# Small loads issued by another queue, squares summed per head, and gate products placed between attention units

## Time and profile before

| | |
|---|---|
| median of three runs | 2365.89 us |
| profiled execution | 2365.77 us |
| its span | 2364.0 us |
| TensorE busy | 1976.3 us (84%) |
| VectorE busy | 414.3 us |
| ScalarE busy | 317.9 us |
| DMA waits in the chain that ended last | 33% of the span |
| TensorE in that chain | 60% |

### The profile page before, as it was taken

One profiled execution on the slowest core, in us unless ns is written; L12 is line 12 of the kernel. 1 busy time (PEld: TensorE's weight loads), 2 busy tenths in 40 slices (PEclk: granted clock), 3 DMA queues, 4 the chain that ended last, 5 costly groups with the idle time before them and its releaser, 6 DMA issues.

```text
span 2364.0 us, 27849 instructions
## 1 busy us (share of the span) xinstructions
PE 1976.3 (84%) x12006; PEld 1249.7 (53%) x12006; DVE 414.3 (18%) x1209; ACT 317.9 (13%) x722; POOL 0.2 (0%) x4
## 2 busy tenths in 40 slices
PE   7999998976666666666666699899999999899999
PEld 4468787521111111111111155778888748588888
DVE  5113333300000000000000033451000105620000
ACT  4132021200000000000000022341000103501000
POOL 0000000000000000000000000000000000000000
PEclk9999998978888788787888899999999999999999
DMA  9146576999999999999999973526434645155341
GB/s 350 66 171 222 187 267 244 404 428 429 428 428 429 428 429 428 428 429 428 429 428 428 425 254 127 187 72 236 156 107 161 216 141 196 61 191 188 131 178 36
DMA packets 147871, 648.45 MB, mean 274 GB/s; under 512 B 10645, under 2 KB 17410, under 8 KB 123016
## 3 DMA queue, kind: packets, MB, share of 16 engines
q1 hardware_dynamic: 141254, 643.16, 68.7%
q10 hardware_dynamic: 6530, 4.01, 0.6%
HBM read 646.10 MB, written 1.05 MB: 274 GB/s over the span
## 4 chain that ended last, share of the span: by engine, by line
PE 60%; DMA 33%; DVE 4%; ACT 1%; issue 1%; SPq 1%; ACTq 1%; DVEq 0%
DMA ring<-in_w_exp 32%; PE bank L823 28%; PE bank L837 6%; PE bank L2309 6%; PE bank L1626 4%; PE bank L1378 4%; PE bank L1641 2%; PE bank L856 1%; DMA ring<-in_w_ada 1%; DVE scr L2204 1%; DVE scr L2221 1%; PE bank L593 1%; PE bank L1303 1%; PE bank L701 1%; PE bank L1312 1%
## 5 line engine op out<-in xcount | busy, mean ns | idle before, releaser
L823 PE MATMUL bank<-hx,ring 128*128 128x256 f32 (+1 forms) x2944 | 655.1, 385 | 0.7 <-ACT hx L719 0.7
L823 PEld LDWEIGHTS bank<-hx,ring 128*128 128x128 f32 x2944 | 560.6, 191 | 92.1 <-issue 19.0
L1626 PE MATMUL bank<-ring,arena 128*32 128x512 f32 x1968 | 304.0, 751 | 208.3 <-DMA ring<-in_w_exp 198.0
L1626 PEld LDWEIGHTS bank<-ring,arena 128*32 128x32 f32 x1968 | 60.6, 124 | 434.1 <-DMA ring<-in_w_exp 315.2
L1641 PE MATMUL bank<-ring,arena 128*32 128x512 f32 x1008 | 162.0, 784 | 80.1 <-DMA ring<-in_w_exp 69.2
L837 PE MATMUL bank<-ring,hx 128*128 128x512 f32 (+1 forms) x384 | 152.9, 561 | 1.4 <-ACT hx L779 0.7
L2309 PE MATMUL bank<-arena,ring 128*128 128x256 f32 x704 | 152.4, 380 | 1.6 <-DVE arena L2342 1.6
L2309 PEld LDWEIGHTS bank<-arena,ring 128*128 128x128 f32 x704 | 133.9, 190 | 19.8 <-issue 2.0
L1641 PEld LDWEIGHTS bank<-ring,arena 128*32 128x32 f32 x1008 | 32.9, 132 | 192.1 <-DMA ring<-in_w_exp 111.1
L837 PEld LDWEIGHTS bank<-ring,hx 128*128 128x128 f32 x384 | 72.9, 190 | 80.2 <-issue 76.1
L1684 DVE COPY arena<-bank 128x256 f32<-128x256 f32 x16 | 6.8, 424 | 524.1 <-PE bank L1631 524.1
(11 more groups left out here) (369 smaller groups left out, 1368.7 us busy)
## 6 DMA issues: line engine op xcount, KB each, us to landing
ring<-in_w_exp SPq DMA_DIRECT2D x186, 2048.0 KB, 16.3
ring<-in_w_ada SPq DMA_DIRECT2D x36, 2048.0 KB, 12.1
ring<-in_w_in SPq DMA_DIRECT2D x29, 2048.0 KB, 9.0
ring<-in_w_ffn_in SPq DMA_DIRECT2D x20, 2048.0 KB, 7.9
ring<-in_w_ffn_out SPq DMA_DIRECT2D x10, 2048.0 KB, 7.8
ring<-in_w_out SPq DMA_DIRECT2D x6, 2048.0 KB, 11.9
arena<-in_w_exp SPq DMA_DIRECT2D x4, 2048.0 KB, 20.2
ring<-in_w_up_nsa SPq DMA_DIRECT2D x2, 2048.0 KB, 9.1
```

The lines of the kernel that those rows point to most:

```text
L823: ins = pe.matmul(b[:, o:o + n], w[:, k, j * P:(j + 1) * P], h[:, k, :], start=k == 0, stop=k == KD - 1)
L1626: ins = pe.matmul(banks[s][32 * j:32 * j + 32, :], e_xe[:, 2 * t + kk, :], w[:, kk, 512 * j:512 * j + 512], start=t + kk == 0, stop=t + kk ...
```

## The change

1. The 20 small loads are issued by SyncE, in the tile list behind `branch_ml` and before the two `out1_` tiles, still after the step "full S3". `pe_rope` stands behind the mixer's products instead of before them, and VectorE's copy of its result (`dve_turn_pe`) behind VectorE's side of the mixer. `dve_rope` keeps its place and its wait for the loads.
2. The squares of the mLSTM heads are summed head by head, one fused instruction behind each piece of `hh`; the product and the reduction over all of it are gone.
3. Gate tiles 2 and 3 of each layer are computed in halves of 32 products: the first half of tile 2 where the tile was, the second behind the head transposes, the first half of tile 3 behind the scores of unit 0, the second behind the compressed scores. The transposed compressed keys follow tile 3's first half. ScalarE applies the sigmoid at once to the first half of tile 2; the other three are copied as they are, and one sigmoid over all six blocks follows the last unit. The order of the first units changes on TensorE (compressed transposes, scores 2, turned 0, scores 3, turned 1, values 0), and on VectorE: maxima of unit 0 go into the compression stage, behind the keys' mean, and unit 0 is normed before the compressed softmax.

The core of the diff:

```diff
@@ pe_branches: - pe_rope(pe);  pe program: + pe_rope(pe) behind m_out[0][0](pe)
@@ act_branches
         act_mlstm_head(act, 3)
-        act_second_loads(act)
-        AC.stage("mlstm")
         act.wait_ge(*at("mlstm mean"))
@@ dve_mlstm
-        sq = view(arena, 16804, P, 8, P)
         hf = hh.rearrange("p c h e -> p (c h) e")
-        v.tensor_tensor(sq, hf, hf, ALU.mult).then_inc(*DV.step())
-        v.wait_ge(*DV.last())
-        v.tensor_reduce(w4[:, 0:8], sq, AX, ALU.add).then_inc(*DV.step())
-        v.wait_ge(*DV.last())
@@ dve_mlstm_out, for each head and half
+            v.wait_ge(*DV.last())
+            v.tensor_tensor_reduce(sqo, hh[:, c, h, :], hh[:, c, h, :], 1.0, 0.0, ALU.mult, ALU.add,
+                                   w4[:, 4 * c + h:4 * c + h + 1]).then_inc(*DV.step())
@@ second loads: act.dma_start -> sp.dma_start, the list is unchanged
+    def dve_turn_pe(v):
+        DV.stage("rope")
+        v.wait_ge(*at("full pet"))
+        v.tensor_copy(pet, bank_of("pet")[0:HD, 0:64]).then_inc(*DV.step("free pet", "pe ready"))
@@ pe_compress
-        pe_gates2(pe, l, 2)
+        pe_gate_half(pe, l, 2, 0)
...
         pe_heads(pe, l)
+        pe_gate_half(pe, l, 2, 1)
...
-        pe_gates2(pe, l, 3)
+
+    def pe_ckeys(pe, l):
         pe.wait_ge(*at(f"kdup{l}"))
@@ act_compress
-        act_gates2(act, l, 2)
+        key = f"gt2{l}20"
+        act.wait_ge(*at("full " + key))
+        act.activation(gates[:, 0:2, 1, :], bank_of(key)[:, :].rearrange("p (j t) -> p j t", j=2), ACT.Sigmoid).then_inc(
+            *AC.step("free " + key))
...
+        act_gate_raw(act, l, 2, 1)
         act.wait_ge(*at(f"cmp mean{l}"))
...
-        act_gates2(act, l, 3)
@@ dve_compress, behind "cmp mean"
+        dve_maxima(v, l, 0)
@@ pe_attend
         scores(0)
+        pe_gate_half(pe, l, 3, 0)
+        pe_ckeys(pe, l)
+        scores(1)
         pe.wait_ge(*at(f"kct ready{l}"))
...
-        scores(1)
+        pe_gate_half(pe, l, 3, 1)
         pe.wait_ge(*at(f"scT{l}"))
...
+        scores(2)
         turned(0)
-        scores(2)
+        scores(3)
         turned(1)
         values(0)
-        scores(3)
@@ act_attend
         probs(0)
+        act_gate_raw(act, l, 3, 0)
...
         probs(1)
+        act_gate_raw(act, l, 3, 1)
...
         copies(LAST)
+        act.wait_ge(*AC.last())
+        act.activation(gates[:, 2:8, 1, :], gates[:, 2:8, 1, :], ACT.Sigmoid).then_inc(*AC.step(f"gates{l + 1}"))
@@ dve_attend
-        softmax_in(0)
         softmax_in(1)
         v.wait_ge(*at(f"head gates{l}"))
+        normed(0)
         v.wait_ge(*at(f"full ct{l}"))
...
-        normed(0)
         softmax_in(2)
@@ new helpers
+    def pe_gate_half(pe, l, t, i):
+        w = tile(pe, f"merge2_{l}{t}0")
+        key = f"gt2{l}{t}{i}"
+        b = bank(pe, key)
+        for j in range(2):
+            for k in range(KD):
+                ins = pe.matmul(b[:, j * N:(j + 1) * N], w[:, k, (2 * i + j) * P:(2 * i + j + 1) * P], h2[:, k, :],
+                                start=k == 0, stop=k == KD - 1)
+        ins.then_inc(*PE.step("full " + key))
+        if i:
+            mark_used(pe, f"merge2_{l}{t}0")
+
+    def act_gate_raw(act, l, t, i):
+        key = f"gt2{l}{t}{i}"
+        act.wait_ge(*at("full " + key))
+        blk = 4 * t + 2 * i - KD
+        act.copy(gates[:, blk:blk + 2, 1, :], bank_of(key)[:, :].rearrange("p (j t) -> p j t", j=2)).then_inc(
+            *AC.step("free " + key))
@@ SyncE
-        for n in range(N_PRE - 4):
+        for n in range(N_PRE - 6):
+            one(n, stream[n])
+        sp_second_loads(sp)
+        for n in range(N_PRE - 6, N_PRE - 4):
             one(n, stream[n])
```

More of the change, by code:

```diff
@@ L914, in pe_branches @@
         pe_mlstm_turn(pe)
-        pe_rope(pe)
     def act_conv(act, i):
@@ L1272, in dve_mlstm @@
                 v.scalar_tensor_tensor(o, b[:, h * P:(h + 1) * P], c_mln[:, h:h + 1], o, ALU.mult, ALU.mult).then_inc(*DV.step(f"free mturn{c}", "yb0"))
+    sqo = arena[:, 18340:18468]
     def dve_mlstm_out(v, h):
@@ L1746, in program, with sp_second_loads @@
     GROUPS = [(0, 8, 0, 0), (768, 2, 8, 1), (KW0, 2, 10, 1), (QB0, 8, 12, 2), (QB0 + 512, 8, 20, 3)]
-    def act_second_loads(act):
-        AC.stage("rope")
-        act.wait_ge(*at("full S3"))
+    def sp_second_loads(sp):
+        sp.wait_ge(*at("full S3"))
         def load(dst, src, **kw):
-            act.dma_start(dst, src, **kw).then_inc(*K.load("load_second"))
+            sp.dma_start(dst, src, **kw).then_inc(*K.load("load_second"))
         pos = A["positions_2"]
@@ L1786, in dve_rope @@
         v.wait_ge(*K.loaded("load_second"))
-        v.wait_ge(*at("full pet"))
-        b = bank_of("pet")
-        v.tensor_copy(pet, b[0:HD, 0:64]).then_inc(*DV.step("free pet", "pe ready"))
         v.tensor_tensor(fold, ident[:, 0:32], ident[:, 32:64], ALU.add).then_inc(*DV.step())
@@ L1990, in dve_compress @@
         v.tensor_scalar(msc[0:15, 0:2], msc[0:15, 0:2], 1.0 / HD, EPS, ALU.mult, ALU.add).then_inc(*DV.step(f"cmp mean{l}"))
+        DV.stage("attend")
+        dve_maxima(v, l, 0)
+        DV.stage("compress")
         g = gain_l[0:15, l, 1, :].rearrange("p (s e) -> p s e", s=2)
@@ L2191, in on_dve, with dve_maxima @@
         return par == 1 and m % 3 == 2
+    def dve_maxima(v, l, m):
+        if m >= 3:
+            v.wait_ge(*at(f"full pt{l}_{m - 3}1"))
+        for par in range(2):
+            key = f"s{l}_{m}{par}"
+            v.wait_ge(*at("full " + key))
+            b = bank_of(key)
+            for c, (lo, hi) in enumerate(((0, P), (P, 3 * P))):
+                v.tensor_tensor_reduce(sm[:, m % 3, par, lo:hi], b[:, lo:hi], causal[:, P:N] if c == 0 else causal[:, :],
+                                       -1.0, 3e38, ALU.add, ALU.min, mx[:, m % 3, par, c:c + 1]).then_inc(
+                    *DV.step("free " + key, f"sm{l}_{m}{par}"))
     def dve_attend(v, l):
@@ L2196, in softmax_in @@
         def softmax_in(m):
-            if m >= 3:
-                v.wait_ge(*at(f"full pt{l}_{m - 3}1"))
-            for par in range(2):
-                key = f"s{l}_{m}{par}"
-                v.wait_ge(*at("full " + key))
-                b = bank_of(key)
-                for c, (lo, hi) in enumerate(((0, P), (P, 3 * P))):
-                    v.tensor_tensor_reduce(sm[:, m % 3, par, lo:hi], b[:, lo:hi], causal[:, P:N] if c == 0 else causal[:, :],
-                                           -1.0, 3e38, ALU.add, ALU.min, mx[:, m % 3, par, c:c + 1]).then_inc(
-                        *DV.step("free " + key, f"sm{l}_{m}{par}"))
+            dve_maxima(v, l, m)
         def normed(m):
@@ L2406, in _ @@
         m_out[0][0](pe)
+        pe_rope(pe)
         n_ffn0[0](pe)
@@ L2482, in _ @@
         m_out[0][1](v)
+        dve_turn_pe(v)
         dve_gain(v, "gain ffn0", gs, c_ffn[:, 0:8], adaX[0][:, 32:40], "adaX0b")
```

## The result

The changed kernel took 2339.1 us (median of four runs, 2338.06 to 2343.72) against 2366.02 before, a ratio of 0.9888 with a 95% interval of 0.9877 to 0.99: 26.9 us less. Run again later beside new runs of before it took 2338.4 (2336.6 to 2338.98), ratio 0.9878, 0.9861 to 0.9894. The forecast was 2343.5, a gain of 22.3.

A forecast was written before the change was run, and what follows sets the result against it. DMA bounds the experts' stretch, whose start TensorE's progress sets; the gains lie in TensorE's idle around it. 7.5 us ahead of the experts plus 14.8 in two attentions made 22.3, hence 2343.5 us, own range 2340 to 2348, wide 2337.5 to 2351.

The forecast's parts named there:

- the two places: TensorE's idle holes at the mLSTM's end and each attention's start: 7.5 us ahead of the experts, 7.4 us per layer.
- The root behind its mean: End of the mLSTM: with the loads off ScalarE, the root follows VectorE's mean at once, saving 3.9 us.
- The guess that the table load would come ahead of the wait: ScalarE's root: its table loads before the wait for the mean, saving 3.9 us; behind it, 2.65.
- The wait for small loads: Ahead of the first merge product: TensorE no longer waits for the small loads, saving 2.9 us.
- the half clock at the mixer's start: Mixer's first products: the 2 us clock loss stays; 2 to 3 us more gain if it vanishes, 2 less if doubled.
- the 0.3 of the moved transposes: Between mixer and norm: the position table's two transposes, moved there, cost about 0.3 us.
- The squares: End of the mLSTM: summing squares per head saves 1.0 us net, between 0 and 1.5.
- The attentions: Start of each layer's attention: 9.1 us gained less 1.7 for half clock, 7.4 per layer, range 5.5 to 9.1.
- The joint sigmoid: End of the attention: table load 1.28 us and sigmoid 1.9 stay hidden, with 6 us to spare.
- rival (a): Clock holds through both attention starts, 1.7 us more each, and perhaps 1 at the mixer: 2339 us; chance 17%.
- Rival (d): SyncE's queue fills: 4 us per small load gives 2388 us, slower than before from 2.9 an issue; chance 4%.
- the limit of 375.5: VectorE's angle work: small loads may land as late as 375.5 us before TensorE stalls for a bank.

The follow-up runs named there:

- the second profile: The changed kernel, unaltered, profiled a second time, later; run again later it took 2338.4 us, ratio 0.9878 to before.
- the halved loads: The changed kernel with each of the 20 small loads issued in two halves by partitions, 40 issues on SyncE; 2341.13 us.
- the table ahead: The changed kernel with the position table's transposes and their copy put back ahead of the first merge product; 2343.69 us.
- the three single parts: Three kernels made from before, each with one part of the change: loads 2360.58 us, squares 2367.39 us, gate halves 2351.07 us.
- quarters: The changed kernel with each of the 20 small loads issued in four pieces, 80 issues on SyncE; 2353.39 us.

## Why the prediction came out as it did

The sign and the two places were right, and the forecast was 4.4 us too high: 2339.1 lies just below the forecast's own 2340 to 2348, inside the wide range of 2337.5 to 2351. By its own terms:

- The root behind its mean, 3.9 booked. From the mean to TensorE's start took 361.07 - 356.19 = 4.88 us before and 357.81 - 356.60 = 1.21 after: 3.7 (3.9 in the second profile). The guess that the table load would come ahead of the wait held (347.65).
- The wait for small loads, 2.9 booked: the merge product had started 370.16 - 367.15 = 3.01 us behind the last gated product and now starts 0.26 behind it: 2.75.
- **The term that was mis-sized is the half clock at the mixer's start.** The forecast kept the whole loss, because TensorE would still idle twice for 2 us, and said that 2 to 3 us more would come if it vanished. From head 3 to the experts 9.25 and 10.05 us were gained, not 7.5. The root and the squares gave 4.8 and 5.1 of that (24.18 us from head 3 to L604 before, 19.35 and 19.10 after; 4.9 booked) and the wait 2.75; what is left is 1.7 and 2.2 us, or 2.0 and 2.5 with the 0.3 of the moved transposes. The idles were there (0.78 and 2.10 us, 1.96 and 1.68), but each time only the transposes or the product ran slow, no longer both.
- The squares, 1.0 booked: 1.16 measured between head 3 and the mean (19.30 to 18.14), with eight instructions of 0.29 as the nearest row had it. The forecast did not say that this term hangs on part one; alone it is zero.
- The attentions, 9.1 - 1.7 booked each. In the first layer unit 1 was turned 5.9 us earlier reckoned from the join (6.0 forecast), the idle was 2.34 (2.5), and unit 4's scores came 9.1 and 8.7 earlier (9.7 without the clock's loss). What reached the end was 8.32 and 8.75, then 8.03 and 7.55, against 7.4. The clock's price was about right: where it fell, in three of the four, the rows behind the idle took 1.5 us more than at full clock. But the forecast took off 0.6 us for VectorE's chain and 1.7 for the clock, and these overlap. In the one attention at full clock TensorE waited 0.75 us for VectorE a unit later, and 0.16 at the same place where the clock had fallen (first profile, then second, both in the second layer):

```profile
2008.69 0.98 PE L2090 MATMUL bank<-ident,scr 128*128 128x128 f32 x6 [0.75 <-DVE scr L2236]
```
```profile
2008.53 0.98 PE L2090 MATMUL bank<-ident,scr 128*128 128x128 f32 x6 [0.16 <-DVE scr L2236]
```

- A slip in the sum: 1542.65 - 1533.7 is 8.95, not 9.1, which would have made the forecast 2343.8.
- The joint sigmoid lay beside other work: 1.49 us, begun at 1550.11, against the first merge product at 1554.36.
- The median of the first series hit rival (a)'s 2339, in part by luck. (a) had the clock hold through both attentions and perhaps 1 us at the mixer; it held in one attention of four, and the mixer gave 2.0 to 2.5. And 0.7 and 1.5 us of the gain lies in stretches without an edit: the end of the experts gave 2.2 and 2.0, and the start of the kernel took 1.6 and 0.6 back. So (a) was right about the clock as the direction of the miss, not about the place.
- Rival (d) was not what happened, since an issue cost 0.72 us (14.5 us for 20). The limits behind it held: at 1.34 us a load no bank wait, at 1.9 us a wait of 9.67, with the loads 10.9 us past the limit of 375.5. That the change turns slower than before at 2.9 us a load was not reached. The price of the expert tiles sent later was missing from it.
- The rule of the Trainium skill that the forecast weighed ("DMA: Bandwidth & Descriptors", Queues, rings and completion order: one ring's descriptors are taken in order) agrees with the trace. The first loads behind the weights landed 8.4 to 10.9 us after issue, at 358.3 to 359.4, with the branch weights landed at 359.1; those issued from 357.5 us on took 2.2 to 3.5. It cost nothing, as said.

Open stays the tail of the experts: from last tile to join 11.12 us before and 8.75 in both profiles of after, in code that no edit touches. This is nearly all of the 2.0 to 2.2 us by which experts to join is shorter. The same 16 products take 3.64 us at half clock or 1.92 at full there. Of the ten profiles of kernels with parts one and three together eight had 8.75 (the others 10.3 with the halved loads, 10.2 with the table ahead), while before and the three single parts all had over 11. The length of the idle ahead of the last tile does not decide it: 2.99 us stood there with the products at full clock (second profile), 1.89 with them at half (before). The cause stays open.

## What to carry to other kernels

Where an engine waits behind a list of issues, what is computed ahead of the wait is worth nothing until the issues are gone: undo the larger cause first, then measure the smaller. Fill ahead of a place where a wait ends, and move the filler's copy out of PSUM along with it, or the bank that it holds becomes the next wait. Where an idle is left, cut a smaller piece: a quarter of 3.6 us in an idle of 2.34 paid. Price each idle removed with the half clock that may follow it. When small transfers move to the queue that feeds a DMA-bound stretch, count the time in which that queue sends no weights, even if everything that waits for the small ones is covered.

## What the runs showed of the hardware

- The issue of a small load does not cost SyncE in proportion to its size: 0.46 us for 128 KB, 0.43 for most of 8 and 32 KB, 1.22 for one of 1 KB; halves mostly 0.60, quarters 0.42, with single ones up to 1.4.
- A table load that stands ahead of the wait cost nothing here: the root's stood at 347.65, 9 us ahead. The sigmoid's took 1.28 us and the function began 0.02 us behind it (1548.81, 1550.11). By the Trainium skill ("ScalarE: Activation LUTs", What ACT_TABLE_LOAD costs) a switch would be 2.66 us with a drain. The copy ahead of it ended at 1548.80, so no such drain shows here.
- The same program's attention, with the same instructions and the same idles, took 192.48, 194.28 and 196.20 us in three kernels (before, loads alone, squares alone) whose differences lie some 1600 us ahead of it. The four idles at its start are equal to 0.01 us (1.86, 2.33, 3.54, 1.15); the rows between and behind them are the same work at half or full clock. That is a spread of 3.7 us from the clock, larger than the squares' term and the wait for the small loads.
- An idle of one length did not decide the clock: behind 2.34 us it fell in three attentions of the changed kernel and held in one.
